# Output projection of a hybrid encoder layer: f32 products replaced by three fp16 products of halves

## What is computed

```
h = rmsnorm(x, ln1_g)
proj = h @ w_in                                   # 1024 -> 3080
out_a = rglru(causal_conv(proj[.., :512])) * gelu(proj[.., 512:1024])      # 512 features
q, k, v = heads(silu(causal_conv(proj[.., 1024:2560])))                    # 4 heads of 128
S, o = gated delta rule over chunks(q, k, v, beta, g)                      # state S, output o
o = rmsnorm(o, gdn_ng) * silu(z)                                           # 512 features
x = x + concat(out_a, o) @ w_out                                           # 1024 -> 1024
x = x + hier_moe(rmsnorm(x, ln2_g))                                        # top-1 group, top-2 experts
y = rmsnorm(x, final_g)
```

## Time and profile before

| | |
|---|---|
| median of 3 runs | 4324.17 us (4323.01 to 4324.24) |
| profiled execution | 4329.62 us, span 4328.0 us, mean granted TensorE clock 0.927 |
| TensorE matmul (PE) busy | 3577.7 us, 83% |
| TensorE weight load (PEld) busy | 2176.8 us, 50% |
| VectorE (DVE) busy | 2200.0 us, 51% |
| ScalarE (ACT) busy | 1679.3 us, 39% |
| GpSimd (POOL) busy | 947.6 us, 22% |
| f32 products of the output projection | L998 251.0 us and L1010 269.6 us, 528 records each |

### The profile page before, as it was taken

How to read it: one execution, slowest core, us unless ns; L and a number is a source line. 1 busy time by engine, 2 the same in 40 slices (tenths; PEclk the granted TensorE clock), 3 DMA queues, 4 the chain that set the end, 5 groups by cost and what they waited for, 6 DMA issues and landing times. The chain is left out here.

```text
span 4328.0 us, 72419 instructions
## 1 busy us (share of the span) xinstructions
PE 3577.7 (83%) x21028; PEld 2176.8 (50%) x21029; DVE 2200.0 (51%) x4880; ACT 1679.3 (39%) x2974; POOL 947.6 (22%) x1046
## 2 busy tenths in 40 slices
PE   8987696886978589899989999998739999999920
PEld 3443343333434567666766766676524444444410
DVE  6566474664756445655655565556432222222257
ACT  6556465564655433333333333333112222222222
POOL 0000000000000123333333334333111111111145
PEclk9998898998989699999999999999869999999965
DMA  4465656656565312121112111221046666774379
GB/s 146 150 207 195 223 191 216 213 198 212 196 202 190 131 35 68 53 65 58 63 53 65 58 63 54 64 68 54 15 185 225 224 231 220 271 269 151 107 293 381
DMA packets 293079, 656.24 MB, mean 152 GB/s; under 512 B 26467, under 2 KB 138595, under 8 KB 292579
## 3 DMA queue, kind: packets, MB, share of 16 engines
q1 hardware_dynamic: 182162, 321.70, 23.4%
q0 software_dynamic: 56512, 186.76, 11.5%
q10 hardware_dynamic: 54288, 146.56, 8.7%
HBM read 404.57 MB, written 250.38 MB: 151 GB/s over the span
## 5 line engine op out<-in xcount | busy, mean ns | idle before, releaser
L341 PE MATMUL pP<-h_hi,w_hi 128*128 128x512 f16 (+1 forms) x1728 | 634.8, 371 | 59.4 <-ACT win L435 40.1
L341 PE MATMUL pP<-h_lo,w_hi 128*128 128x512 f16 (+1 forms) x1728 | 634.6, 371 | 0.0
L341 PE MATMUL pP<-h_hi,w_lo 128*128 128x512 f16 (+1 forms) x1728 | 632.8, 370 | 0.0
L1631 PE MATMUL ebank<-ws_sb,rowsT 128*128 x2352 | 528.3, 382 | 40.0 <-issue 39.0
L1631 PEld LDWEIGHTS ebank<-ws_sb,rowsT 128*128 128x128 f16 x2352 | 229.4, 98 | 313.7 <-issue 67.6
L542 DVE SCALAR_TENSOR_TENSOR halves<-stage,halves 128x1024 f16<-128x1024 f32 x192 | 234.5, 1222 | 248.5 <-ACT halves L411 248.5
L293 POOL DMA_DIRECT2D ws<-halves x192 | 103.2, 537 | 1122.1 <-DVE halves L542 615.8
L577 DVE SCALAR_TENSOR_TENSOR cv<-win,cols_sb,cv 128x512 f32<-128x512 f32 (+1 forms) x432 | 305.5, 707 | 33.9 <-issue 0.9
L1247 DVE TENSOR_TENSOR WI<-bank,const 128x512 f32<-128x512 f32 x198 | 136.5, 690 | 351.6 <-PE bank L919 347.1
L341 PEld LDWEIGHTS pP<-h_hi,w_hi 128*128 128x128 f16 x1728 | 174.3, 101 | 256.2 <-ACT win L435 44.6
L411 ACT ACTIVATE halves<-stage 128x1024 f16<-128x1024 f32 x192 | 201.9, 1052 | 259.8 <-POOLq L296 255.7
(11 more groups left out here) (290 smaller groups left out, 6036.3 us busy)
## 6 DMA issues: line engine op xcount, KB each, us to landing
stage<-in_we SPq DMA_DIRECT2D x192, 512.0 KB, 4.1
ws<-halves POOLq DMA_DIRECT2D x192, 512.0 KB, 3.9
ws_sb<-ws SPq DMA_DIRECT2D x32, 3072.0 KB, 13.7
y<-yb ACTq DMA_DIRECT2D x98, 512.0 KB, 4.7
ft<-mixin SPq DMA_DIRECT2D x33, 1280.0 KB, 6.1
mixin<-qo ACTq DMA_DIRECT2D x128, 256.0 KB, 2.8
xt<-in_x SPq DMA_DIRECT2D x33, 512.0 KB, 5.9
xr<-in_x SPq DMA_DIRECT2D x33, 512.0 KB, 4.8
```

The costliest lines, as they stand in the source:

```text
L341: ins = nc.tensor.matmul(pP[n % NPB][:, 0:N], w[:, k, c0:c0 + P], h[:, k, 0:N], start=(k + i == 0), stop=(k == KD - 1 and i == 2))
L1631: ins = nc.tensor.matmul((M0, M1)[p][:, :], xT[p][:, x, k, :], half(s, k // 2, w, k % 2 * 512), start=(k + i == 0), stop=(k == KD - 1 and ...
```

## The change

`w_out` is held as two fp16 tiles, `w_out_hi` and `w_out_lo`, scaled by 512. The features get halves too, scaled by 4: `f_hi`, `f_lo` for the recurrent ones (new steps `fh` on ScalarE and `fl` on VectorE) and `mx_hi`, `mx_lo` for the others (`mh` on ScalarE, `ml` on VectorE). Each of the 16 products becomes three fp16 products of halves (hi by hi, lo by hi, hi by lo) into the same bank. `x2` scales the sum back while it adds the residual. `fh` and `fl` are the last steps of the X part, `mh` and `ml` stand between `mx` and `outB0`. `outA1` moves behind Z2, and `outB0` moves behind T4, next to `outB1`. The wait of `load` for `outA1` goes away.

The split of `w_out` runs once: its raw halves are loaded into `kz` and `S_s`, and after the first run ScalarE makes eight pieces of `w_out_hi`, VectorE eight of `w_out_lo`. SP waits for `w_out_ready` ahead of the load of `S_s`, and the loads of the loop stand behind that.

```diff
+M_SCALE = 4.0
+OUT = 1.0 / (W_SCALE * M_SCALE)
...
 X.W2.pe X.I2.dve Y.outA0.pe
-X.T2.pe X.T2c.act Y.outA1.pe Y.oT.pe X.B8.pool
-X.W4.pe X.Z2.pe X.Z2c.act Y.mx.dve X.I4.dve Y.outB0.pe X.B16.pool
-X.T4.pe X.T4c.act Y.outB1.pe X.B32.pool
+X.T2.pe X.T2c.act Y.oT.pe X.B8.pool
+X.W4.pe X.Z2.pe X.Z2c.act Y.mx.dve Y.mh.act X.I4.dve Y.outA1.pe Y.ml.dve X.B16.pool
+X.T4.pe X.T4c.act Y.outB0.pe Y.outB1.pe X.B32.pool
...
-X.Z64.pe X.Z64c.act
+X.Z64.pe X.Z64c.act X.fh.act X.fl.dve
...
+        w_out_raw = [kz[:, :, :, :].rearrange("p h s n -> p (h s n)").rearrange("p (k n) -> p k n", k=4),
+                     S_s[:, :, :, :].rearrange("p s h n -> p (s h n)").rearrange("p (k n) -> p k n", k=4)]
...
             last = NT - 1
             run((0, 0, False), None, None)
+            if after_first:
+                after_first()
             run((1, 1, False), (0, 0, False), None)
...
-                sp.wait_ge(*at("outA1", t, 2))
                 sp.wait_ge(*at("mx", t, 2))
                 sp.dma_start(ft[p][:, :, :], T["mixin"][:, :, bass.ts(t, P)]).then_inc(ft_in[p], 16)
...
-            sp.dma_start(w_out[:, :, :], T["w_out"]).then_inc(w_out_in, 16)
+            for n, half in enumerate(w_out_raw):
+                sp.dma_start(half, T["w_out"][:, n * 4:n * 4 + 4, :]).then_inc(w_out_in[n], 16)
+            sp.wait_ge(w_out_ready, KD)
             sp.dma_start(S_s[:, :, :, :], T["S_s"]).then_inc(S_s_in, 16)
...
-                        pe.wait_ge(w_out_in, 16)
-                    pe.wait_ge(*at("x2", t, 1))
+                        pe.wait_ge(w_out_ready, KD)
+                    pe.wait_ge(*at("fl", t))
                     pe.wait_ge(*at("r0" if half == 0 else "hc1", t, 1))
                     for c in (2 * c0, 2 * c0 + 1):
-                        ins = nc.tensor.matmul(flat((YD, YE)[half]), ft[p][:, QC + ZC + c, :],
-                                               w_out[:, c, half * 512:half * 512 + 512], start=(c == 0), stop=False)
+                        for i, (w, f) in enumerate(((w_out_hi, f_hi), (w_out_lo, f_hi), (w_out_hi, f_lo))):
+                            ins = nc.tensor.matmul(flat((YD, YE)[half]), f[:, c, :],
+                                                   w[:, c, half * 512:half * 512 + 512], start=(c + i == 0), stop=False)
                     ins.then_inc(*did(n))
...
-                    pe.wait_ge(*at("mx", t))
+                    pe.wait_ge(*at("ml", t))
                     half, h = divmod(int(n[-1]), H)
-                    nc.tensor.matmul(flat((YD, YE)[half]), mx[:, h, :], w_out[:, LC + h, half * 512:half * 512 + 512],
-                                     start=False, stop=(h == H - 1)).then_inc(*did(n))
+                    for i, (w, f) in enumerate(((w_out_hi, mx_hi), (w_out_lo, mx_hi), (w_out_hi, mx_lo))):
+                        ins = nc.tensor.matmul(flat((YD, YE)[half]), f[:, h, :],
+                                               w[:, LC + h, half * 512:half * 512 + 512],
+                                               start=False, stop=(h == H - 1 and i == 2))
+                    ins.then_inc(*did(n))
                 elif n in ("hT0", "hT1"):
...
+                elif n == "fh":
+                    act.wait_ge(ft_in[p], ft_turn(t, p))
+                    act.wait_ge(*at("outA1", t, 1))
+                    nc.scalar.activation(f_hi[:, :, :], ft[p][:, QC + ZC:FC, :], ACT.Copy, scale=M_SCALE).then_inc(*did(n))
...
+                elif n == "mh":
+                    act.wait_ge(*at("outB7", t, 1))
+                    act.wait_ge(*at("mx", t))
+                    nc.scalar.activation(mx_hi[:, :, :], mx[:, :, :], ACT.Copy).then_inc(*did(n))
...
+            def split_out():
+                for k in range(KD):
+                    act.wait_ge(w_out_in[k // 4], 16)
+                    nc.scalar.activation(w_out_hi[:, k, :], w_out_raw[k // 4][:, k % 4, :], ACT.Copy, scale=W_SCALE
+                                         ).then_inc(w_out_hi_ready, 1)
+
+            program("act", act, x_step, y_step, split_out)
...
+                elif n == "fl":
+                    dve.wait_ge(*at("fh", t))
+                    nc.vector.scalar_tensor_tensor(f_lo[:, :, :], ft[p][:, QC + ZC:FC, :], M_SCALE, f_hi[:, :, :],
+                                                   ALU.mult, ALU.subtract).then_inc(*did(n))
...
+                    dve.wait_ge(*at("mh", t, 1))
+                    nc.vector.scalar_tensor_tensor(mx[:, :, :], YC[:, :, :], ng4[:, 0:1], ft[p][:, QC:QC + ZC, :],
                                                    ALU.mult, ALU.mult).then_inc(*did(n))
+                elif n == "ml":
+                    dve.wait_ge(*at("mh", t))
+                    nc.vector.tensor_tensor(mx_lo[:, :, :], mx[:, :, :], mx_hi[:, :, :], ALU.subtract).then_inc(*did(n))
                 elif n == "x2":
...
-                    nc.vector.tensor_tensor(x2b[:, 0:512], flat(YD), xr[p][:, 0:512], ALU.add)
-                    nc.vector.tensor_tensor(x2b[:, 512:], flat(YE), xr[p][:, 512:], ALU.add).then_inc(*did(n))
+                    nc.vector.scalar_tensor_tensor(x2b[:, 0:512], flat(YD), OUT, xr[p][:, 0:512], ALU.mult, ALU.add)
+                    nc.vector.scalar_tensor_tensor(x2b[:, 512:], flat(YE), OUT, xr[p][:, 512:], ALU.mult, ALU.add
+                                                   ).then_inc(*did(n))
...
+            def split_out():
+                for k in range(KD):
+                    dve.wait_ge(w_out_hi_ready, k + 1)
+                    nc.vector.scalar_tensor_tensor(w_out_lo[:, k, :], w_out_raw[k // 4][:, k % 4, :], W_SCALE,
+                                                   w_out_hi[:, k, :], ALU.mult, ALU.subtract).then_inc(w_out_ready, 1)
+
+            program("dve", dve, x_step, y_step, split_out)
```

More of the change, by code:

```diff
@@ L685, in mix_phase @@
         const = sb("const", [P, NMAT, P])
-        w_out = sb("w_out", [P, KD, D])
+        w_out_hi = sb("w_out_hi", [P, KD, D], FP16)
+        w_out_lo = sb("w_out_lo", [P, KD, D], FP16)
+        f_hi = sb("f_hi", [P, LC, P], FP16)
+        f_lo = sb("f_lo", [P, LC, P], FP16)
+        mx_hi = sb("mx_hi", [P, H, P], FP16)
+        mx_lo = sb("mx_lo", [P, H, P], FP16)
+        ng4 = sb("ng4", [P, 1])
         router = sb("router", [P, KD, P])
@@ L767, in mix_phase @@
         weights_in = sem("mix_weights_in")
-        w_out_in = sem("w_out_in")
+        w_out_in = [sem(f"w_out_in{n}") for n in range(2)]
+        w_out_hi_ready = sem("w_out_hi_ready")
+        w_out_ready = sem("w_out_ready")
         S_s_in = sem("S_s_in")
@@ L797, in col, with program @@
             return cols[:, COLS[name][0] + n:COLS[name][0] + n + w]
-        def program(engine, begin, x_step, y_step):
+        def program(engine, begin, x_step, y_step, after_first=None):
             for (st, e), d in done.items():
@@ L1121, in y_step @@
                     nc.scalar.activation(exd[:, NGR:], dif[:, NGR:], ACT.Exp).then_inc(*did(n))
-            program("act", act, x_step, y_step)
+            def split_out():
[4 more added lines that the diff above has]
+            program("act", act, x_step, y_step, split_out)
         @block.gpsimd
@@ L1308, in y_step @@
                     dve.wait_ge(*at("oT", t))
-                    nc.vector.scalar_tensor_tensor(mx[:, :, :], YC[:, :, :], col("ng"), ft[p][:, QC:QC + ZC, :],
+                    dve.wait_ge(*at("mh", t, 1))
+                    nc.vector.scalar_tensor_tensor(mx[:, :, :], YC[:, :, :], ng4[:, 0:1], ft[p][:, QC:QC + ZC, :],
                                                    ALU.mult, ALU.mult).then_inc(*did(n))
+                elif n == "ml":
+                    dve.wait_ge(*at("mh", t))
+                    nc.vector.tensor_tensor(mx_lo[:, :, :], mx[:, :, :], mx_hi[:, :, :], ALU.subtract).then_inc(*did(n))
                 elif n == "x2":
@@ L1405, in _ @@
             dve.sem_inc(x2_out, 16)
+            nc.vector.tensor_scalar(ng4[:, :], col("ng"), M_SCALE, None, ALU.mult)
             dve.drain()
-            program("dve", dve, x_step, y_step)
+            def split_out():
[4 more added lines that the diff above has]
+            program("dve", dve, x_step, y_step, split_out)
             dve.drain()
```

## The result

| | before | after |
|---|---|---|
| median | 4324.2 us (4323.01 to 4327.73, 4 runs) | 4367.4 us (4365.50 to 4369.79, 4 runs) |
| ratio | | 1.0099, 95% interval 1.0081 to 1.0116 |
| profiled execution | 4329.62, span 4328.0 | 4369.79, span 4368.1 |
| granted TensorE clock, mean | 0.927 | 0.931 |

Slower by 43 us; 87 were forecast, and 4411 stood against 4367. The sign was right, the size was not, and the range (from 4374) misses it.

The account below looks back on a forecast made before the run. The prediction took a chain of latencies, not TensorE's work, to bound the kernel. Turn +65, start +26, middle -8, end -1.5 and clock +5 gave +86.5; 4329.6 + 86.5 - 5.4 = 4411 us, range 4374 to 4452.

Parts of the forecast that it names:

- the range (from 4374): Whole kernel: measured time expected between 4374 and 4452 us, with about 0.15 of the chance left outside.
- TensorE has waits, not too much work: Ladder: copy latencies set its length, so nearly all the 3.4 us of TensorE time freed per tile falls into waits.
- The rival that gave 4238: Whole kernel: TensorE is the bound after all, so freed product time counts, giving 4238 us; chance 0.04.
- Turn, +65: Turn of the tile: fl ahead of gs and xb delays the VectorE path 2.1 us in each of 31 turns.
- Start, +26: Start of phase: splitting w_out and queued loads delay tile 1, and TensorE returns at half clock; together +26 us.
- My 23 and 3: Start of phase: +23 us for the later sq of tile 1, +3 for TensorE's half clock after idling.
- Middle, -8: T2 to W8: 0.6 us gained in 16 tiles, 0.1 lost in 16 others where GpSimd slows ml; -8 us.
- In the other kind of tile: Middle, about every second tile, with onb at 1.76: ml runs alone and W8 comes 0.6 us earlier.
- such a flip: Before T2: GpSimd and VectorE order changing so all tiles are one kind, moving time 18 us either way.
- Clock, +5: Around T2: thinner TensorE work brings three more clock falls of 1.7 us; +5 us, from -5 to +20.
- End, -1.5: Last Y, with no X to hide behind: outB saves 1.7, mh and ml cost 1.3, outA saves about 1.

Follow-up runs that it names:

- e4: The changed kernel with two fp16 products in place of three (high weights by low features left out); a tile gets 0.43 us shorter.
- e1: The changed kernel with fh and fl moved from the turn to behind T16's copy in the ladder; median 25.5 and 29.0 us below the changed kernel's two.
- e5: The kernel before, products still f32, with fh and fl added at the turn and their results unread; median +38 us.
- e2: The changed kernel with the wait for w_out's split and the load of S_s behind all tile loads; start 70.2 to 55.1 us, median 8 to 12 lower.
- e8: The changed kernel run again unaltered for a second profile; profiled span 4377.5 us.
- c1: The changed kernel with fh, fl behind T8's copy, S_s loaded last, B4 behind onb, and outA and outB products moved; 4257 us, 1.5% faster than before.
- c3: c1 with outB0 to outB5 one gap earlier, outB6 alone, and B16 held until ml is done; 2.0% below the kernel before.
- e6: The kernel before with one added wait: GpSimd begins B4 only after VectorE finishes onb; 55 us gained.
- c2: The kernel before, all f32, with B4 behind onb, outA0 behind outA3 and outA1 behind W2; 2.0% below the kernel before.

## Why the prediction was right in sign and wrong in size

- **TensorE has waits, not too much work**: shown. 3.4 us freed per tile gain nothing (T8 to T16 4.12 after, 4.13 before), and two of sixteen products show in e4. The rival that gave 4238 is out for this kernel.
- **Turn, +65**: right in place and nearly in size. xb 1.96 later, xn 1.95, not 2.1: the scalar_tensor_tensor form of x2b costs nothing (0.68, as the plain form). 31 x 1.95 is 60.5, and one of the 31 lies behind the last KS. e1 and e5 show it by taking it away and by adding it to the kernel before.
- **Start, +26**: right, +25.4, of which e2 takes 15.1 back by the queue's order alone. My 23 and 3 split it as the trace does: sq of tile 1 starts 24.2 after KS of tile 0 instead of 0.8, and its sixteen records at half clock lost 1.7.
- **Middle, -8**: here is the step that failed: "In the other kind of tile [...] T2 is 1.1 us later against the same B steps, ml runs alone, outB0 starts 5.3 after T2, W8 6.6 after T2: 0.6 earlier." It took the order of GpSimd's and VectorE's operations as given. In its place T2 comes 2.25 us sooner after T1 in nearly every tile of this kind (13 of 15, and 14 in e8), and `ml` is blocked in all steady tiles (median 1.32). T1 to W8 lost 2.13 there instead of 0.6. That is 1.5 x 15 = 23 us. The order changed because VectorE's idle of 0.19 us ahead of `dif` is gone from the changed program (read from the traces; no run moves the idle alone). e5 gives half of it (T1 to T2 7.14) with the f32 products in place; e1 never has the slow order, with no delay at the turn. The prediction named such a flip last among what would make it wrong, at 18 us for all tiles of one kind, but gave it no chance of its own, and did not know of the arrangement that came, 1.1 us faster than the faster of its two kinds. Had the flip stood among the rivals, a range from 4356 would have held the time.
- **Clock, +5**: wrong sign. The prediction expected more falls from thinner work around T2. The four falls stood at the long wait before T2, which the flip removed, and after has none; neither has e5, whose products are f32 and whose long wait is gone. That gave -6.6 (four of 1.65) instead of +5, so it belongs to the same step.
- **End, -1.5**: +3.0 measured from the last KS on (1322.4 in e8 against 1319.4). 2.0 of it is the last of the 31 turns (T1 comes 19.65 after that KS instead of 17.67); e5, which has the turn and f32 products, is 2.5 longer there. So the last Y itself costs about 1 us instead of saving 1.5. In c1 and c3, with the products elsewhere and no turn, the stretch is 0.9 and 0.1 longer than before. Which step pays the 1 us was not tried by itself.
- **Sum.** Against e8, whose first inverse took as long as before's: +25.4 start, +20.0 tiles (15 pairs x 1.71 = 25.7, less 6.6 for the falls, and 0.9 more, most of it the one tile that took 7.07 from T1 to T2), +3.0 end, +1.1 ahead of the phase's first `sq`: 49.5, the difference of the spans (4377.5 and 4328.0). In place of 86.5: -23 for the flip, -11.6 for the clock, -4.5 for the turn, +2.5 at the end, which gives 49.9. The profile of after lies 10 us lower by the level of the clock in the first inverse, and the medians (43 and 49 apart) carry a part of that.

What stays open: why VectorE's idle stands ahead of one `esel` in every second tile of the kernel before and ahead of none after, why B4 starts 0.08 us later in every second tile, who wins when B4 is 20 to 30 ns ahead of `dif`, and why the first inverse gets one level of the clock in one execution and the other in the next.

## What to carry to other kernels

Before pricing a change, look for places where two engines that block each other start within 0.1 us. Instructions added elsewhere in an engine's program can change who comes first there, and that may give back or cost as much as the change itself, so such a flip needs a chance and a price. Fixing the order with one wait (B4 behind `onb`) gained 55 us here, more than the cheaper products did in any arrangement. Work that a cheaper operand form needs (halves, splits) goes where its engine waits anyway, and a one-time load that is needed last goes last in its queue.

## What was not expected of the hardware

- A 128x1 VectorE operation of 0.15 us takes 1.23 us, and one of 128x4 1.27 instead of 0.21, when GpSimd's 128x512 operation started 20 to 100 ns before. With the second `dif` 20 to 30 ns behind it, GpSimd's took 1.90 and `onb` 0.68 in most tiles, and GpSimd's 1.31 and `onb` 1.77 in others with the same starts.
- VectorE idles 0.19 us, put down to issue, ahead of the same small operation in every second tile of before, e6 and c2, and ahead of none of these operations in the eight profiles of the changed kernel and its variants.
- The same kernel's first inverse ran at a granted clock of 0.99 (the 2.4 GHz level) in one execution and 0.50 (the 1.2 GHz level) in another, 41.3 and 51.8 us from `sq` to KS of tile 0.
